# Routed experts of a transformer kernel: slot table and output rows stored by position, then expert, with one load for the slot numbers of experts 8 to 63

## The reference, cut to what matters

```python
T, D = x2d.shape                                  # 512, 1024
scores = sigmoid(x2d @ w_router)                  # 64 experts
...                                               # best 4 of 8 groups, then top 8
w = take_along_axis(scores, top_idx, axis=1)
w = w / sum(w, axis=-1, keepdims=True) * 2.5
...
def swiglu(x, w_gu, w_down):
    g, u = split(x @ w_gu, 2, axis=-1)            # 1024 -> 2 x 256
    return (silu(g) * u) @ w_down                 # 256 -> 1024
out = swiglu(x_pad[tok], w_exp_gu[e], w_exp_down[e])   # for the tokens of expert e
routed = zeros.at[tok].add(out * w)
return routed + swiglu(x2d, w_sh_gu, w_sh_down)        # shared expert
```

## Time and profile before

| what | value |
|---|---|
| median of 3 runs | 2232.14 us |
| the profiled execution, its own time | 2227.5 us |
| its span in the trace | 2225.7 us |
| mean granted TensorE clock | 0.969 of full speed |
| PE busy | 2032.3 us (91%) |
| DVE, ACT, POOL busy | 772.3, 472.6, 335.4 us |
| DMA queue q1 (SP) | 45216 packets, 300.95 MB |
| DMA queue q10 (ACT) | 16496 packets, 32.45 MB |
| DMA queue q0 (POOL) | 12832 packets, 33.63 MB |
| packets under 512 B | 18336 of 74610 |

### The profile page before, as it was taken

The page is one execution under the profiler, slowest core; times in us unless marked ns, Lnnn a source line. Parts: engine busy times, 40 slices in busy tenths (PEclk is TensorE's granted clock), DMA queues, the critical chain, the costliest instruction groups (busy, mean ns, idle before and its releaser), DMA issues.

```text
span 2225.7 us, 26064 instructions
## 1 busy us (share of the span) xinstructions
PE 2032.3 (91%) x10002; PEld 933.2 (42%) x10002; DVE 772.3 (35%) x1604; ACT 472.6 (21%) x1043; POOL 335.4 (15%) x353
## 2 busy tenths in 40 slices
PE   7888999999996899898888899699988899999997
PEld 3324434445442343333333334344745444444443
DVE  5998771223281233222222233701265300000012
ACT  2234421100210233232222221211244000000000
POOL 0653250000034211111111102400023000000000
PEclk9998999999998999999999999899999999999999
DMA  5110014213245999999999995803310122222210
GB/s 222 47 38 1 18 68 150 76 37 149 79 152 189 325 378 381 374 375 362 364 360 362 364 344 183 309 14 142 124 38 1 64 78 76 76 76 76 76 38 28
DMA packets 74610, 367.92 MB, mean 165 GB/s; under 512 B 18336, under 2 KB 18592, under 8 KB 57648
## 3 DMA queue, kind: packets, MB, share of 16 engines
q1 hardware_dynamic: 45216, 300.95, 37.1%
q0 software_dynamic: 12832, 33.63, 4.6%
q10 hardware_dynamic: 16496, 32.45, 4.0%
HBM read 345.95 MB, written 29.42 MB: 169 GB/s over the span
## 4 chain that ended last, share of the span: by engine, by line
PE 67%; DMA 17%; DVE 9%; issue 4%; POOL 1%; ACT 1%; another core or an unknown queue 1%; ACTq 0%; POOLq 0%; SPq 0%; DVEq 0%
PE bank L925 41%; PE bank L1256 10%; DMA ring<-w_exp_down 8%; PE bank L1466 6%; DMA slab<-w_exp_down 4%; PE bank L934 2%; DMA s5x<-slot_table 2%; DVE slab L1887 1%; DVE slab L1890 1%; PE bank L1328 1%; DMA slab<-x_rows,s5x 1%; DVE s5x L1887 1%; DVE work L1884 1%; PE bank L1064 1%; PE bank L1274 1%
## 5 line engine op out<-in xcount | busy, mean ns | idle before, releaser
L925 PE MATMUL bank<-slab,ring 128*128 128x512 f32 (+1 forms) x1488 | 632.5, 586 | 13.0 <-DMA ring<-stream 11.3
L925 PEld LDWEIGHTS bank<-slab,ring 128*128 128x128 f32 x1488 | 282.3, 191 | 358.2 <-issue 355.6
L1256 PE MATMUL bank<-slab 128*32 128x512 f32 x1536 | 237.4, 617 | 31.6 <-DMA ring<-w_exp_down 24.3
L1256 PE MATMUL bank<-ring,slab 128*32 128x512 f32 x1536 | 239.2, 614 | 25.3 <-DMA slab<-w_exp_down 17.9
L925 PE MATMUL bank<-ring,slab 128*128 128x512 f32 (+1 forms) x608 | 252.8, 576 | 3.7 <-ACT slab L1499 1.9
L2329 DVE COPY slab<-bank 32x512 f32<-32x512 f32 x124 | 80.9, 688 | 450.5 <-PE bank L1264 402.1
L1264 PE MATMUL bank<-ring,slab 128*32 128x512 f32 x512 | 237.0, 618 | 0.0
L1887 DVE TENSOR_TENSOR slab<-bank,slab 96x256 f32<-96x256 f32 (+3 forms) x120 | 63.8, 532 | 473.0 <-PE bank L925 296.3
L1264 PE MATMUL bank<-slab 128*32 128x512 f32 x480 | 219.5, 612 | 0.0
L925 PEld LDWEIGHTS bank<-ring,slab 128*128 128x128 f32 x608 | 115.5, 191 | 137.5 <-issue 129.7
L2545 POOL TENSOR_TENSOR small<-small 128x1 f32<-128x1 f32 (+2 forms) x30 | 23.0, 766 | 913.9 <-DVE small L1884 913.8
(11 more groups left out here) (275 smaller groups left out, 2163.7 us busy)
## 6 DMA issues: line engine op xcount, KB each, us to landing
ring<-stream SPq DMA_DIRECT2D x171, 512.0 KB, 3.6
slab<-w_exp_gu SPq DMA_DIRECT2D x32, 2048.0 KB
ring<-w_exp_gu SPq DMA_DIRECT2D x32, 2048.0 KB
ring<-w_exp_down SPq DMA_DIRECT2D x32, 1024.0 KB
slab<-w_exp_down SPq DMA_DIRECT2D x32, 1024.0 KB
y_rows<-slab ACTq DMA_DIRECT2D x64, 384.0 KB
gb<-rows ACTq DMA_DIRECT2D x5, 512.0 KB, 5.3
slab<-x_fm SPq DMA_DIRECT2D x1, 2048.0 KB, 9.2
```

The lines of the kernel that those rows point to most:

```text
L925: mm = nc.tensor.matmul(dst, lhs[k], rhs[k], start=(k == 0), stop=(k == len(lhs) - 1))
L1256: mm = nc.tensor.matmul(g_bank[32 * g:32 * g + 32, :], x[:, k, 32 * g:32 * g + 32], w[:, 512 * k:512 * k + 512], start=(k == 0), stop=(k = ...
```

## The change

Both DRAM arrays are laid out as rows of 65 places: place e of row r is position r of expert e, and place 64 is spare. There are 6 times 96 such rows; the first 96 hold what fits an expert's own block, and an overflow block of an expert is rows 96 to 191, and so on. The diff, cut to its core:

```diff
+NCHUNK = 6
+PITCH = 65
+NROW = NCHUNK * CAP * PITCH
...
-        ctrl_i = ctx.enter_context(nc.sbuf_tensor("ctrl_i", [1, 64], I32))
-        slot_tok = s5x[0:CAP, 3072:3076].bitcast(I32)
-        zero_i = s5x[0:CAP, 3200:3200 + NBLK].bitcast(I32)
+        ctrl_i = s5x[0:1, 3200:3328].bitcast(I32)
+        slot_tok = s5x[0:CAP, 3072:3072 + NE].bitcast(I32)
+        no_token = s5x[0:120, 3072:3072 + NROW // 120].bitcast(I32)
+        tab2 = scratch["tab"].rearrange("(r e) o -> r (e o)", e=PITCH)
+        y3 = scratch["y"].rearrange("(r e) d -> r e d", e=PITCH)
```

SP (before the `late` loads), and ACT:

```diff
             down_rows(3, 3)
+            sp.wait_ge(gathered[0], 16)
             for x in late:
...
+            def index_column(e):
+                act.wait_ge(ids_sent[e], 16 * NT)
+                act.dma_start(slot_tok[:, e:e + 1], tab2[0:CAP, e:e + 1], allow_slow_non_contiguous=True).then_inc(idx_landed[e], 16)
             for c in range(2):
                 full("sg", c)
                 nc.scalar.activation(shsig[c], tile("sg", c)[:, :], ACT.Silu).then_inc(act_evac, 1)
+                if c == 0:
+                    index_column(0)
...
-                act.dma_start(scratch["y"][bass.ds(e * CAP, CAP), :], ye[b][0:CAP, :]).then_inc(y_stored[b], 16)
+                act.dma_start(y3[0:CAP, bass.ds(e, 1), :].rearrange("r e d -> r (e d)"), ye[b][0:CAP, :]).then_inc(y_stored[b], 16)
...
-            index_column(0)
             index_column(1)
             x_copy(0, xtr_full, 1, xe_ready)
             index_column(2)
             for b in range(4):
+                index_column(b + 3)
                 e_block(0, b)
-                index_column(b + 3)
-            act.wait_ge(ids_sent[TOPK - 1], 16 * NT)
+            index_column(TOPK - 1)
+            act.dma_start(slot_tok[:, TOPK:NE], tab2[0:CAP, TOPK:NE]).then_inc(idx_rest, 16)
             with act.Fori(1, NE // 4 - 1) as u:
                 for b in range(4):
-                    act.dma_start(slot_tok[:, (b + 3) % 4:(b + 3) % 4 + 1],
-                                  scratch["tab"][bass.ds((4 * u + b + 3) * CAP, CAP), :]).then_inc(idx_landed[(b + 3) % 4], 16)
                     e_block(u, b, first=1)
-            index_column(NE - 1)
```

DVE: eight operations between `pos` and `yrow` become one; the overflow count moves behind the routing weights, and the control words get the first row of each overflow block as well:

```diff
-            link(ts(ovn, cnt, 1.0 / CAP, -(0.5 + 0.5 / CAP), ALU.mult, ALU.add))
...
-            stt(v3(cmp_a), v3(pos), CAP - 0.5, b64(detour), ALU.is_gt, ALU.mult)
-            tt(v3(cmp_b), v3(pos), b64(place), ALU.add).then_inc(dve_evac, 1)
-            dve.wait_ge(dve_evac, plan.done("pos", 0))
-            link(tt(yrow, cmp_a, cmp_b, ALU.add))
+            n = mark(stt(v3(yrow), v3(pos), float(PITCH), b64(iota), ALU.mult, ALU.add))
+            ts(ovn, cnt, 1.0 / CAP, -(0.5 + 0.5 / CAP), ALU.mult, ALU.add).then_inc(dve_evac, 1)
+            dve.wait_ge(dve_step, n)
...
             for j in range(0, NOV, half_n):
...
                 link(nc.vector.tensor_reduce(be[:, j:j + half_n], bc, AX, ALU.add))
+                link(tt(bc, bc, per_block(ovn), ALU.mult))
+                link(nc.vector.tensor_reduce(br[:, j:j + half_n], bc, AX, ALU.add))
```

POOL: the table's preset grows from 96 x 106 to 120 x 312 numbers, 96 spare rows of `y_rows` are set to zero at the same place, and the gathers are written out:

```diff
+            pool.dma_start(y3[0:CAP, NE, :], a["zeros"].broadcast_to([CAP, D])).then_inc(y_pad, 16)
...
-            def gather(u, b, n=None):
-                e = 4 * u + b
-                pool.wait_ge(idx_landed[b], 16 * u + 16)
...
-                if n is None:
-                    pool.wait_ge(idx_ready, e + 1 - TOPK)
-                    nc.gpsimd.tensor_tensor(spare, minus_half[:, 0:1], minus_half[:, 0:1], ALU.mult).then_inc(idx_ready, 1)
...
+            def gather(e):
+                if e < TOPK:
+                    pool.wait_ge(idx_landed[e], 16)
+                elif e == TOPK:
+                    pool.wait_ge(idx_rest, 16)
+                if e >= 2:
+                    pool.wait_ge(gathered[e % 2], 16 * (e // 2))
+                    pool.wait_ge(xtr_full, e - 1)
+                pool.indirect_dma_start(xg[e % 2][0:CAP, :], None, scratch["x2"], ...
...
-            for e in range(TOPK):
+            for e in range(NE):
                 if e + 1 < TOPK:
                     scatter_ids(e + 1)
-                gather(e // 4, e % 4, e)
+                gather(e)
...
-            with pool.Fori(TOPK // 4, NE // 4) as u:
-                for b in range(4):
-                    gather(u, b)
```

More of the change, by code:

```diff
@@ L743, in build @@
         route_init, route_mask, route_addr, route_ctrl = sem("route_init"), sem("route_mask"), sem("route_addr"), sem("route_ctrl")
-        ids_sent, idx_ready = [sem(f"ids_sent{k}") for k in range(TOPK)], sem("idx_ready")
-        idx_landed, idx_ov = [sem(f"idx_landed{j}") for j in range(4)], sem("idx_ov")
+        ids_sent = [sem(f"ids_sent{k}") for k in range(TOPK)]
+        idx_landed, idx_rest, idx_ov = [sem(f"idx_landed{j}") for j in range(TOPK)], sem("idx_rest"), sem("idx_ov")
         gathered = [sem("gathered0"), sem("gathered1")]
@@ L871, in _ @@
             with sp.If(n_ov > 0):
-                sp.dma_start(scratch["y"][NE * CAP:, :], a["zeros"].broadcast_to([NOV * CAP, D])).then_inc(y_zeroed, 16)
-                sp.wait_ge(y_zeroed, 16)
+                n = CAP * PITCH
+                for c in range(1, NCHUNK):
+                    sp.dma_start(scratch["y"][c * n:(c + 1) * n, :], a["zeros"].broadcast_to([n, D])).then_inc(y_zeroed, 16)
+                    sp.wait_ge(y_zeroed, 16 * c)
                 with sp.Fori(0, NOV) as o:
                     with sp.If(n_ov > o):
-                        sp.dma_start(slot_tok[:, 0:1], scratch["tab"][bass.ds((o + NE) * CAP, CAP), :]).then_inc(idx_ov, 16)
                         e = sp.value_load(ctrl_i[0:1, bass.ds(o, 1)], min_val=0, max_val=NE - 1)
+                        r = sp.value_load(ctrl_i[0:1, bass.ds(o + 64, 1)], min_val=CAP, max_val=(NCHUNK - 1) * CAP)
+                        sp.dma_start(slot_tok[:, 0:1], tab2[bass.ds(r, CAP), bass.ds(e, 1)], allow_slow_non_contiguous=True).then_inc(idx_ov, 16)
                         sp.dma_start(gu_w[0], a["w_exp_gu"][bass.ds(e, 1)].rearrange("a p n -> p (a n)")).then_inc(ov["w"], 16)
@@ L2735 @@
         "x2": nc.dram_tensor("x2_rows", (T, D), F32).ap(),
-        "y": nc.dram_tensor("y_rows", (NBLK * CAP, D), F32).ap(),
-        "tab": nc.dram_tensor("slot_table", (NBLK * CAP, 1), I32).ap(),
+        "y": nc.dram_tensor("y_rows", (NROW, D), F32).ap(),
+        "tab": nc.dram_tensor("slot_table", (NROW, 1), I32).ap(),
     }
```

64 lines of the change are left out of this document (29 added, 35 removed).

## The result

The changed kernel takes 2178.89 us (median of 4 runs, 2176.67 to 2183.61), the kernel before took 2231.47 us beside it (4 runs, 2229.28 to 2232.18): a ratio of 0.9769, 95% interval 0.9751 to 0.9787. The profiled execution took 2178.47 us with a span of 2176.6 us (before 2227.5 and 2225.7 us).

The account below looks back on a forecast made before the run. The prediction took full DMA engines to bound the expert stage from about 725 to 1335 us. Start 6.5, slot loads 3 and shorter PE waits 0.5 make 10 us: 2232.14 to 2222 us, range 2212 to 2232 us.

Parts of the forecast that it names:

- Slot loads: In the full DMA stretch, removing 56 loads of slot numbers saves only their packets' engine time, 3 us.
- Rival 3: In the expert loop, each slot load's tiny packets hold up weights by 0.5 us: 28 us, giving 2198 us; chance 0.06.
- Start: At the experts' start, earlier expert 0 products cut idle DMA time and move the full stretch forward: 6.5 us.
- irregular stop: Around expert 0's products, PE stood still for some 6 us, waiting for nothing that the profile names.
- SP's wait: At the experts' start, SP holds weights until the first gather lands; the first slot load meets empty queues, landing at 667.1 us.
- case with the stop: At the experts' start, PE's 6 us standstill stays: idle DMA time 16.1 us, an earlier start worth 5.7 us.
- strided stores: In the full stretch, output stores go to 96 rows 266,240 bytes apart with 4096-byte packets: cost taken as 0.
- rival 2: In the full stretch, 64 stores of 96 spaced rows run slower: 2255 us at 1.5 times, 2289 at twice; chance 0.08.
- ACT's earlier wait for scatter 3: At the experts' start, ACT waits for scatter b + 3 before block b rather than behind it: nothing to 1 us.
- longer control words: At the experts' start, DVE's additional operations free it at about 689 instead of 682 us and add some 1 us to POOL's scatters.
- lock-out: At the start, DVE could block GpSimd's descriptor writing for 12 us, pushing gather 1 and expert 0 back by up to 6 us.
- Rival 4: After 725 us DMA stays unsaturated and PE fixes the end: start gain 13 us, 2216 us; chance within the forecast's 0.72.

Follow-up runs that it names:

- repaired kernel before: The kernel before with all 64 slot loads issued four blocks earlier, into eight columns instead of four, so no gather waits for one: 2196.34 us, 0.9856.
- gathers held: The changed kernel with one slot-column load per block back, into unread columns, and gathers of experts 8 to 62 waiting for their expert's load: 2223.20 us, 0.9955.
- tiny packets back: The changed kernel with 60 loads of one slot column issued again, into columns nobody reads, no gather waiting for them: 2184.41 us, 0.9793.
- gathers in the middle: The changed kernel with gathers of experts 8 to 63 also waiting for the first half of the block's down products: 2222.03 us, 0.9956.
- both in the middle: The changed kernel with gathers and output stores both placed behind the first half of the block's down products: 2192.59 us, 0.9835.
- plain loads: The changed kernel with gathers waiting for the first half of the down products, replaced for experts 8 to 63 by plain loads of 96 rows: 2220.03 us, 0.9946.
- old order: The changed kernel with the previous order of SP's and ACT's loads and waits at the experts' start; the shorter DVE chain stays: 2184.90 us, 0.9796.
- without SP's wait: The changed kernel without SP's wait for the first gather ahead of expert 1's weights: 2180.90 us, 0.9762.
- late-gather run: The changed kernel with gathers of experts 8 to 63 also waiting for the gate and up products of expert e - 3: 2195.74 us, 0.9836.
- short gathers: The changed kernel with gathers of experts 8 to 63 fetching 4 rows instead of 96: 2159.40 us, 0.9689.

## Why the prediction was wrong

**The failed step** is in the prediction's first paragraph: "a wait there for anything else costs nothing while loads are queued", and POOL's 474.2 us of waits for slot loads, "which looks like the item to win, but it lies inside the full DMA stretch, where only the bytes count". The engines were full, but 367 GB/s was not their limit for these bytes. The waits held each gather until the stores' packets were through, and so set the mix in which the packets ran: 318 GB/s in 0.44 of the time. The row was dismissed by a rule about waits when it was a row about placement. Size: 32.7 us (the repaired kernel before), 36 to 38.8 us (gathers held against the same loads unwaited).

**Slot loads:** 3 us predicted from their packets. Two pairs of medians, 2184.41 - 2178.89 and 2196.34 - 2191.11, give 5.5 and 5.2 us, but their intervals are as wide, and the first pair has another cause in it. The run with the tiny packets back has PE stand still once for 8.1 us near 720 us, and was behind by 800 us already; the changed kernel, then this run, then PE's wait of this run from 690 to 730 us:

```profile
655.00:800.00 145.00, 128.74 (x1043) 53.01 (x1045) 54.58 (x126) 33.32 (x76) 48.23 (x47) 0.94 0.81 299
```
```profile
655.00:800.00 145.00, 122.95 (x993) 51.19 (x991) 53.48 (x123) 31.27 (x72) 47.25 (x46) 0.92 0.76 287
```
```profile
PE bank L1265 <- issue: 8.1, 1, 8.1
```

That is 1.7 MB, 4.4 us at 392 GB/s. A wait of this kind, 5.1 to 6.1 us long, stands in the same stretch of three runs without such loads (gathers in the middle, both in the middle, plain loads), so it is not the loads'. In the full stretch the loads take 2 GB/s in both pairs (392 to 390, 391 to 389), 0.5% or 3 us of 600: the predicted size fits. Rival 3 had the outcome nearest to the truth (2198 us, rate beyond 375) for the wrong reason: the loads cost through the wait on them, not by holding up weights.

**Start:** predicted 6.5 us. The milestones came as written, the sum behind them too small. From 655 to 750 us the DMA share rose from 0.60 to 0.70, 9.5 us of idle time saved instead of 5.7 to 7.0 net, and 5.1 MB more were through, 13 us at 392 GB/s, the step's upper bound; the last few us of it are argued to be the better rate again, which no run shows apart. The repaired kernel before agrees: it moved 17.7 MB by 750 us (186 GB/s), 5.7 MB or 14.5 us less than the changed one, and is 17.5 us slower. With the old order it is 2.9 MB or 7.5 us less, but the median is only 6.0 us slower, with intervals that overlap, and the profiled execution 2.4 us. So the order is worth some 6 us by the medians and less by the profile; what the rest of the 13 us comes from is open, since the shorter chain on DVE was not run alone. The irregular stop of 6 us behind expert 0's products was misread as PE standing still: from 701.6 to 708.5 us PE is busy for 5.28 us, but with 20 matmuls only, where expert 0's products had 48 in 8.77 us (some records may be missing).

```profile
701.60:708.50 6.90, 5.28 (x20) 1.25 (x23) 0.00 (x0) 0.00 (x0) 3.50 (x4) 1.00 0.17 40
```

In the changed kernel it comes behind expert 1's products and is 3.3 us (702.46 to 705.74 us, 1.2 us of them turnings); without SP's wait SP's next refill goes out at 707.12 us, 6.7 us behind the end of expert 0's products. What the stop is stays open. The working has one slip: with its own times, the case with the stop has idle parts of 13.8, 0.4 and 2.3 us, not 1.9, which makes the gain 5.3 instead of 5.7 us and changes nothing. What was overrated is SP's wait: it moves the products by 6 us and the end by nothing that can be told from none.

**The sum, with what was measured:** 13 (start, its upper bound) + 3 to 5 (slot loads) + 33 to 39 (gathers beside stores) + 1 (tail) = 50 to 58 us, against 52.6. The terms are not quite apart: the start's and the gathers' share the better rate before 750 us.

**Costs:** strided stores 0, as taken (at most 0.3%), and rival 2 falls. ACT's earlier wait for scatter 3, taken at "nothing to 1 us", held its copy of expert 1's turned rows from 685.5 to 688.36 us, 3 us, but within expert 0's products (to 694.56 us), so nothing was late by it. Beside DVE's longer control words one scatter took 2.23 us, more than the 1.49 us of before; the lock-out that the prediction weighed did not push expert 0 back. Rival 4 has something in it: with the gathers gone PE is the bound, and in the changed kernel it isn't far.

The Trainium skill, page DMA: Bandwidth & Descriptors, section Queues, rings and completion order, says that each DMA engine takes the queues that have work in turn, a packet at a time. By that alone the moment of a gather changes the order of packets and not their sum; the runs, 363 to 392 GB/s with the same bytes per block, show that this isn't the whole of it. Why weights plus one stream of 4096-byte reads move less than weights plus that stream plus writes, no run here tells.

## What to carry to other kernels

A DMA share of 1.00, as at 363 and at 392 GB/s here, does not say that the rate is the best for these bytes: cut one period of the loop into stretches by which queues are active and read GB/s in each. A small load that lands late can set when a large one runs; prefetch the index some blocks deeper (four here) before redesigning its layout. If a loop has weights, a read of small rows and a write-back, try the order in which the read's packets fall beside the write-back's, and look at the packets again after each change of the order.

## What the hardware showed that was not expected

- At a DMA share of about 1.00 the engines moved 318 to 348 GB/s with weights and 4096-byte row reads where such steps were frequent, with weights alone mostly 390 to 400 (357 to 424 over all kernels), with weights and stores 400 to 427 where frequent, with all three 370 to 403. One case stands out: in the late-gather run gather-only steps, with gate and up weights alone beside them, moved 370; why is open.
- A share of 1.00 stood at 386 GB/s in a stretch where PE waited for no load (short gathers): the share alone does not show that the loads limit a stage.
- The gathers' mean packet took 0.197 us in the slow kernels and 0.167 us in the fast ones, 4096 bytes each; the stores' changed the other way, from 0.163 to 0.172 us.
- PE's granted clock from 800 to 1250 us was 0.97 before, a mean of its two levels (1.2 and 2.4 GHz), where PE waited up to 4.3 us for weights, and 1.00 after, where the longest such wait was 1.8 us. It does not explain the rate (377 against 400 GB/s from 800 to 935 us, at 1.00 in both); whether it cost time behind 935 us no run separates.
